# A hybrid block that starts on the residual before the norm between the two models: folded gains, two roots inside the first pair of weight chunks, sums of squares on VectorE, and one more weight chunk split ahead

## The reference, cut to what matters

```python
# end of first_block
h = h + conv_ffn(rmsnorm(h, f_norm_g[l]), ...)
x = rmsnorm(h, final_norm_g)                 # "fin1" in the kernel

# start of second_block
h = x
hn = rmsnorm_2(h, attn_norm[0])              # "at_norm0" in the kernel
proj = hn @ hyb_w_in[0]                      # 14 weight chunks, "hy"
qa, ka, va, rw = split(proj)                 # rw feeds rwkv7_time_mix
h = h + sb_rwkv_mixer(...)                   # needs x itself as the residual
```

## Time and profile before

| what | value |
|---|---|
| median of 3 runs | 1323.04 us (1322.97 to 1324.91) |
| the profiled execution | 1323.27 us, of which the profile's span is 1321.5 us |
| TensorE busy | 1300.0 us, 98% of the span |
| VectorE busy | 913.0 us, 69% |
| ScalarE busy | 758.1 us, 57% |
| GpSimd busy | 44.1 us, 3% |

### The profile page before, as it was taken

How to read it: one execution, slowest core, us unless ns; L and a number is a source line. 1 busy time by engine, 2 the same in 40 slices (tenths; PEclk the granted TensorE clock), 3 DMA queues, 4 the chain that set the end, 5 groups by cost and what they waited for, 6 DMA issues and landing times.

```text
span 1321.5 us, 29315 instructions
## 1 busy us (share of the span) xinstructions
PE 1300.0 (98%) x12222; PEld 1268.0 (96%) x12222; DVE 913.0 (69%) x1297; ACT 758.1 (57%) x977; POOL 44.1 (3%) x37
## 2 busy tenths in 40 slices
PE   9999999999999999999999999999999999999997
PEld 8999999998899999999989899999999889999997
DVE  4789886488479876468746387666578779666556
ACT  6667665367657665357554166554476876554444
POOL 1010000010010000010000010000001001000000
PEclk9999999999999999999999999999999999999999
DMA  8455555545345555535401135555435335555520
GB/s 333 175 208 191 191 190 191 191 191 195 125 160 191 191 190 191 191 122 191 160 34 37 65 136 211 182 184 199 179 141 187 130 128 200 192 190 190 191 96 33
DMA packets 31981, 220.63 MB, mean 167 GB/s; under 512 B 3712, under 2 KB 3840, under 8 KB 6160
## 3 DMA queue, kind: packets, MB, share of 16 engines
q1 hardware_dynamic: 30672, 213.36, 44.7%
q0 software_dynamic: 784, 4.85, 1.1%
q10 hardware_dynamic: 432, 1.05, 0.2%
HBM read 218.20 MB, written 1.05 MB: 166 GB/s over the span
## 4 chain that ended last, share of the span: by engine, by line
PE 87%; DVE 8%; ACT 3%; issue 1%; DMA 1%; POOL 0%; SPq 0%; DVEq 0%; ACTq 0%; POOLq 0%
PE ps L1850 22%; PE ps L1851 21%; PE ps L1852 21%; PE ps L1861 17%; DVE w_lo L1102 2%; PE ps L1856 2%; PE ps L1857 2%; PE ps L1858 2%; ACT w_hi L503 1%; DVE xt L1154 1%; PE ps L2072 1%; DMA raw<-stream 1%; DVE xA L1164 1%; DVE xB L1164 0%; DVE xB L1126 0%
## 5 line engine op out<-in xcount | busy, mean ns | idle before, releaser
L1102 DVE TENSOR_TENSOR w_lo<-raw,w_hi 128x2048 fp32r<-128x2048 f32 x197 | 449.9, 2288 | 149.3 <-ACT w_hi L503 148.8
L503 ACT ACTIVATE w_hi<-raw 128x2048 fp32r<-128x2048 f32 x197 | 376.2, 1913 | 169.8 <-PE ps L1852 165.4
L1850 PE MATMUL ps<-xB,w_hi 128*128 128x256 f32 x1120 | 314.4, 281 | 1.7 <-DVE up_acc L1228 1.7
L1852 PE MATMUL ps<-xB,w_lo 128*128 128x256 f32 x1120 | 312.7, 279 | 0.0
L1851 PE MATMUL ps<-xB,w_hi 128*128 128x256 f32 x1120 | 312.6, 279 | 0.0
L1850 PEld LDWEIGHTS ps<-xB,w_hi 128*128 128x128 f32 x1120 | 210.5, 188 | 3.1 <-DVE up_acc L1228 1.9
L1850 PE MATMUL ps<-xA,w_hi 128*128 128x256 f32 x744 | 210.7, 283 | 0.5 <-DVE w_lo L1102 0.5
L1851 PEld LDWEIGHTS ps<-xB,w_hi 128*128 128x128 f32 x1120 | 210.5, 188 | 0.1
L1852 PEld LDWEIGHTS ps<-xB,w_lo 128*128 128x128 f32 x1120 | 210.5, 188 | 0.0
L1851 PE MATMUL ps<-xA,w_hi 128*128 128x256 f32 x744 | 207.7, 279 | 0.0
L1852 PE MATMUL ps<-xA,w_lo 128*128 128x256 f32 x744 | 207.6, 279 | 0.0
(11 more groups left out here) (295 smaller groups left out, 1909.3 us busy)
## 6 DMA issues: line engine op xcount, KB each, us to landing
raw<-stream SPq DMA_DIRECT2D x199, 1024.0 KB, 4.8
raw<-stream SPq DMA_DIRECT2D x4, 512.0 KB, 7.6
at_bias<-rel POOLq DMA_DIRECT2D x1, 2048.0 KB, 8.1
hT<-x_t SPq DMA_DIRECT2D x4, 256.0 KB, 7.0
lora_w<-lora POOLq DMA_DIRECT2D x1, 1024.0 KB, 5.1
out_t<-xt SPq DMA_DIRECT2D x4, 256.0 KB, 2.4
hcon<-hyc POOLq DMA_DIRECT2D x1, 576.0 KB, 4.0
wsT<-wst ACTq DMA_DIRECT2D x1, 512.0 KB, 4.4
```

Source lines behind the costliest of these rows:

```text
L503: nc.scalar.activation(w_hi[c.slot][:], raw[c.slot][:], ACT.Copy).then_inc(hi_made, 1)
L1102: nc.vector.tensor_tensor(w_lo[c.slot][:], raw[c.slot][:], w_hi[c.slot][:].bitcast(F32), ALU.subtract).then_inc(lo_made, 1)
L1850: nc.tensor.matmul(out, wh, xh, start=start, stop=False, skip_group_check=True)
L1852: return nc.tensor.matmul(out, wl, xh, start=False, stop=stop, skip_group_check=True)
```

## The change

The separate norm `N_FIN1` goes. The hybrid block's pair and third chunk work on the old `hT` times `hy_gain`, the product of both norm weights. ScalarE makes two sets of squares for each quarter of `hT`: of `hT`, and of `hT * fin1` (eight more activations into `slot[2]` and `slot[3]`). VectorE adds both sets down (six additions; GpSimd adds nothing for this norm), TensorE sums both inside the pair, now at k = 6 rather than 5. The first root `fin_rs` comes from the first sum; VectorE multiplies the second sum by `fin_rs` squared; ScalarE takes the second root; VectorE multiplies the two roots into `rs`. The matmuls on ones go. `split_hi` and `split_lo` for `c0+4` move ahead of the block's evacuations, and the residual itself is normed (eight products into `hT`) between `with_eye(10, ...)` and `with_eye(14, ...)`.

```diff
-N_GM, N_FF0, N_AT, N_FF1, N_FIN1, N_HY, N_FF2, ... = range(12)
+N_GM, N_FF0, N_AT, N_FF1, N_HY, N_FF2, ... = range(11)
+POOLED = {n: 0 if n == N_HY else 2 if n in FOLDED else 1 for n in range(11)}
+        def early_gain(n, k):
+            return hy_gain[:, k:k + 1] if n == N_HY else col(EARLY[n][0], k)
 # GpSimd
-            add_squares(N_FIN1)
             pool.wait_ge(h_updated, 16)
...
-            add_squares(N_HY)
 # ScalarE
             ffn(1, N_FF1)
-            square_norm(N_FIN1)
             for b in range(4):
                 square(N_HY, b)
+                for k in (2 * b, 2 * b + 1):
+                    last = nc.scalar.activation(slot[2 + k // 4][:, k % 4, :], hT[:, k, :], ACT.Square, scale=col("fin1", k))
+                last.then_inc(fin_sq, 1)
             split_hi(Chunk(c0).ahead())
-            root_norm(N_HY)
+            act.wait_ge(ss_summed, N_HY + 1)
+            inverse_root(fin_rs[:], half(4, 0), D, fin_made)
+            act.wait_ge(fin_mean, 1)
+            inverse_root(rs[:], rs[:], 1, rs_made)
+            split_hi(Chunk(c0 + 1).ahead())
             round_x(OUT_HY, xA)
...
             act.wait_ge(mu_ready, 1)
-            split_hi(Chunk(c0 + 1).ahead())
             hy_copy(0)
 # VectorE, end of ffn
+                if n + 1 == N_HY:
+                    for b in (0, 4):
+                        dve.wait_ge(sq_made, 4 * N_HY + b // 2 + 2)
+                        own.mark(nc.vector.tensor_tensor(xt[:, b + 2:b + 4, :], xt[:, b + 2:b + 4, :], xt[:, b:b + 2, :],
+                                                         ALU.add))
+                    own.wait()
+                    nc.vector.tensor_tensor(xt[:, 6:8, :], xt[:, 6:8, :], xt[:, 2:4, :], ALU.add).then_inc(sq_folded, 1)
+                    dve.wait_ge(fin_sq, 4)
+                    for i in (2, 3):
+                        own.mark(nc.vector.tensor_tensor(slot[i][:, 0:2, :], slot[i][:, 0:2, :], slot[i][:, 2:4, :], ALU.add))
+                    own.wait()
+                    nc.vector.tensor_tensor(slot[2][:, 0:2, :], slot[2][:, 0:2, :], slot[3][:, 0:2, :],
+                                            ALU.add).then_inc(fin_folded, 1)
                 split_lo(Chunk(d0 + PAIRS - 1).ahead())
 # VectorE, around the hybrid block
+            link(nc.vector.tensor_tensor(hy_gain[:, 0:KD], col("fin1", 0, KD), col("at_norm0", 0, KD), ALU.mult))
             ffn(1, N_FF1)
-            root(N_FIN1)
-            for k in range(KD):
-                ins = nc.vector.scalar_tensor_tensor(out=hT[:, k, :], in0=hT[:, k, :], scalar=col("fin1", k), in1=rs[:],
-                                                     op0=ALU.mult, op1=ALU.mult)
-                ...
-            nc.vector.tensor_scalar(om_mu[:], ...).then_inc(mu_ready, 1)
-            dve.wait_ge(h_updated, 20)
-            for b in range(4):
-                rest_early(N_HY, b)
-            fold_squares(N_HY)
-            c0 = C0["hy"]
-            split_lo(Chunk(c0).ahead())
+            dve.wait_ge(fin_made, 1)
+            link(nc.vector.scalar_tensor_tensor(out=rs[:], in0=half(4, 1), scalar=1.0 / D, in1=fin_rs[:], op0=ALU.mult,
+                                                op1=ALU.mult))
+            nc.vector.tensor_tensor(rs[:], rs[:], fin_rs[:], ALU.mult).then_inc(fin_mean, 1)
+            split_lo(Chunk(c0).ahead())
+            nc.vector.tensor_scalar(om_mu[:], ...).then_inc(mu_ready, 1)
             root(N_HY)
+            link(nc.vector.tensor_tensor(rs[:], rs[:], fin_rs[:], ALU.mult))
             scale_x(OUT_HY, xA, "at_norm0")
+            split_lo(Chunk(c0 + 1).ahead())
...
             scale_early(N_HY, 2, c0 + 2, 2)
-            split_lo(Chunk(c0 + 1).ahead())
             shift(2)
...
             split_lo(Chunk(c0 + 12).ahead())
+            for k in range(KD):
+                nc.vector.scalar_tensor_tensor(out=hT[:, k, :], in0=hT[:, k, :], scalar=col("fin1", k), in1=fin_rs[:],
+                                               op0=ALU.mult, op1=ALU.mult).then_inc(fin_scaled, 1)
             with_eye(14, 7, -1)
 # TensorE, sum_folded and the block
-                plain(half(4, 0), ones, xt[:, 7, :], False, True).then_inc(ss_summed, 1)
+                last = plain(half(4, 0), ones, xt[:, 7, :], False, True)
+                if n == N_HY:
+                    pe.wait_ge(fin_folded, 1)
+                    plain(half(4, 1), ones, slot[2][:, 0, :], False, False)
+                    last = plain(half(4, 1), ones, slot[2][:, 1, :], False, True)
+                last.then_inc(ss_summed, 1)
...
-            keep_clock(10, 3)
-            sum_quarters(N_FIN1, range(4))
...
-                    early_pair(N_HY, Chunk(c0), Chunk(c0 + 1), 5)
+                    early_pair(N_HY, Chunk(c0), Chunk(c0 + 1), 6)
```

More of the change, by code:

```diff
@@ L75 @@
 OUT_GATED, OUT_FF0, OUT_KV, OUT_Q, OUT_FF1, OUT_HY, OUT_FF2, OUT_PL0, OUT_FF3, OUT_PL1 = range(10)
-N_GM, N_FF0, N_AT, N_FF1, N_FIN1, N_HY, N_FF2, N_PL0, N_ML, N_FF3, N_PL1, N_FIN2 = range(12)
+N_GM, N_FF0, N_AT, N_FF1, N_HY, N_FF2, N_PL0, N_ML, N_FF3, N_PL1, N_FIN2 = range(11)
 EARLY = {N_GM: ("a_norm", 4), N_FF0: ("f_norm0", 2), N_AT: ("kv_norm", 3), N_FF1: ("f_norm1", 2), N_HY: ("at_norm0", 3),
@@ L83 @@
 SCALED_AT = {n: sum(c for m, (_, c) in EARLY.items() if m < n) for n in EARLY}
-FOLDED = tuple(n for n in range(12) if n not in (N_FIN1, N_FIN2))
-ADDED_BY = {n: sum(2 if m in FOLDED else 1 for m in range(n)) for n in range(12)}
+FOLDED = tuple(range(N_FIN2))
+POOLED = {n: 0 if n == N_HY else 2 if n in FOLDED else 1 for n in range(11)}
+ADDED_BY = {n: sum(POOLED[m] for m in range(n)) for n in range(11)}
 FOLD_AT = {n: i for i, n in enumerate(FOLDED)}
 FINAL_XT = 8 * 10
-FILL = (3, 9)
 GATE_BANK = (4, 6, 7, 5)
@@ L143, in build @@
         rs = sb("rs", [P, T])
+        hy_gain = sb("hy_gain", [P, 4 * KD])
         with ExitStack() as f:
@@ L211, in build @@
                 om_mu = sb("om_mu", [P, 15], where=f)
+                fin_rs = sb("fin_rs", [P, T], where=f)
                 slot = [sb(f"slot{i}", [P, RBLK, T], where=f) for i in range(12)]
@@ L264, in build @@
         rs_made = sem("rs_made")
+        fin_sq, fin_folded, fin_made, fin_mean, fin_scaled = [
+            sem(n) for n in ("fin_sq", "fin_folded", "fin_made", "fin_mean", "fin_scaled")]
         xt_made = sem("xt_made")
@@ L477, in _ @@
             add_squares(N_FF2)
-            pool.wait_ge(h_updated, 24)
+            pool.wait_ge(h_updated, 20)
             pool.dma_start(pl_in[:], p_t[0]).then_inc(p_landed, 16)
@@ L486, in _ @@
             add_squares(N_FF3)
-            pool.wait_ge(h_updated, 36)
+            pool.wait_ge(h_updated, 32)
             pool.dma_start(pl_in[:], p_t[1]).then_inc(p_landed, 16)
@@ L1153, in scale_x @@
                 for k in range(KD):
-                    nc.vector.scalar_tensor_tensor(out=xt[:, k, :], in0=hT[:, k, :], scalar=col(gain, k), in1=rs[:],
+                    nc.vector.scalar_tensor_tensor(out=xt[:, k, :], in0=hT[:, k, :],
+                                                   scalar=early_gain(N_HY, k) if o == OUT_HY else col(gain, k), in1=rs[:],
                                                    op0=ALU.mult, op1=ALU.mult).then_inc(xt_made, 1)
@@ L1281, in ffn @@
                     rest_early(n + 1, 3)
-                if n + 1 in FOLDED:
+                if n + 1 in FOLDED and n + 1 != N_HY:
                     fold_squares(n + 1)
+                if n + 1 == N_HY:
[11 more added lines that the diff above has]
+                                            ALU.add).then_inc(fin_folded, 1)
                 split_lo(Chunk(d0 + PAIRS - 1).ahead())
@@ L1678, in _ @@
                 dve.wait_ge(chunk_used, co + g + 1)
+                if g == 0:
+                    dve.wait_ge(fin_scaled, KD)
                 add_quarter(g, 4 + g)
@@ L1870, in keep_clock, with sum_quarters @@
                     plain(ps[:, bank, 0:P], ones, ones)
-            def sum_quarters(n, quarters, idle=True):
+            def sum_quarters(n, quarters):
                 for b in quarters:
@@ L1879, in sum_quarters @@
                     else:
-                        if b == 3 and idle:
-                            keep_clock(FILL[0])
                         pe.wait_ge(sq_made, 4 * n + b + 1)
@@ L1886, in sum_quarters @@
                     last.then_inc(ss_summed, 1)
-                    if idle:
-                        keep_clock(FILL[1])
             in_halves = Chunk(0), Chunk(1)
@@ L2541, in _ @@
             keep_clock(12)
-            sum_quarters(N_FIN2, (2, 3), idle=False)
+            sum_quarters(N_FIN2, (2, 3))
 def _cols(v):
```

7 lines of the change are left out of this document (3 added, 4 removed).

## The result

The changed kernel takes 1331.35 us, the median of six runs (1327.48 to 1333.32), where the kernel before takes 1323.91 (1322.97 to 1324.91): a ratio of 1.0047, 95% interval 1.0033 to 1.0061. The forecast was 1317.1 us and faster. The profiled execution took 1327.48 us, its span is 1325.7. It is the fastest of the six: it lies 4.2 us above the profiled execution before, the median 7.4 us above the median before, so what follows accounts for 4.2 us and the rest of the median's loss is in no profile.

A forecast was written before the change was run, and what follows sets the result against it. TensorE, busy 98%, was taken to bound the kernel. Of 11.8 us without useful matmuls, gaps of 1.0, 1.5, 2.4 and a 0.7 sum return; 6.1 gained: 1323.27 - 6.1 = 1317.2, median 1317.1, range 1314.7 to 1319.1.

The forecast's parts named there:

- ScalarE's pace: First quarters of `hT`: two roundings, a square and two gained squares take ScalarE 2.16 us a quarter, setting the pace.
- `scale_x` held by the split of `c0+3`: Behind the roots: VectorE's `split_lo` of `c0+3`, 581.3 to 583.5, not the root, sets `scale_x` at 584.0, before 588.90.
- the split of `c0+4` between it and the banks: Behind `scale_x`: VectorE's `split_lo` of `c0+4` adds 2.2 us, so `scale_early` comes at 592.1, only 2.7 us earlier.
- the waits for the first and the fourth shift: TensorE: `c0+4` waits for the first shift until 594.6, the `lora_w` products for the fourth until 602.6.
- The eight late products: Products into `hT`, 3.25 us, done at 712.6: covered with 0.7 us left; with this placing they cost 0 to 1.
- the 6.04: Measured gain in us from the first quarter's addition to the `lora_w` products; the forecast for this stretch was 6.1.
- three gaps: TensorE's waits between second feed-forward and `lora_w` products, before the second sum, `c0+4` and those products: forecast 1.0, 1.5, 2.4 us.
- What is at no cost: Prediction's part on covered work: late products into `hT`, `hy_gain` (at most 0.2 us of `scale_early`'s delay), and transfers.
- the other side: Slower case: the clock falls at the third gap and stays at half; at 20 us it gives 1327; chance 0.04.
- a time between 602.6 and the block's end: Sign of being wrong: from the `lora_w` products to the hybrid block's end, times not the old ones moved by 6.1 us.
- no spell of half clock: TensorE's clock behind the new order's gaps: full clock assumed; one spell would cost 1.7 us, leaving 4.4 us gained.
- rival 1: One spell of half clock after the new order's third TensorE gap: 4.4 us gained, 1318.9; chance 0.12.

The follow-up runs named there:

- old_all_shifted: The kernel before with 128 unused bytes per partition ahead of the weight buffers, so weights and activations both lie 128 bytes higher; ratio 1.0006.
- old_96: The kernel before with 64 unused bytes behind the roots, so activations lie 96 bytes above the weights modulo 256; ratio 1.0199.
- new_again: The changed kernel repeated without alteration, beside the others on one chip; 1329.59 us, ratio 1.0051 to the kernel before.
- new_unshifted: The changed kernel with the `hy_gain` tile placed behind the hybrid block's slots, so no tile ahead of that block moves; 1321.15 us, ratio 0.9984.
- new_filled: new_unshifted with 26 small matmuls on ones in TensorE's three gaps; 1319.64 us, ratio 0.9971 to the kernel before.
- new_f17: new_unshifted with 17 small matmuls on ones in TensorE's three gaps (2, 5 and 10); 1320.03 us, ratio 0.9963 to the kernel before.
- new_f17_late9: new_f17 with nine more small matmuls on ones directly ahead of the third feed-forward; 1319.49 us, ratio 0.9961 to the kernel before.
- new_f17_mid9: new_f17 with nine more small matmuls on ones ahead of the first of the 64x64 products; 1319.89 us, ratio 0.9970 to the kernel before.

## Why the prediction was wrong

**What was right.** The chain of the changed place, step by step: ScalarE's pace, the pair without a gap at its start, the additions of 0.60 and 0.68 us, `scale_x` held by the split of `c0+3`, the split of `c0+4` between it and the banks, the waits for the first and the fourth shift. From the first addition `scale_x` starts at 19.65 us (forecast 584.0 - 564.28 = 19.7) and the banks are scaled at 27.69 (27.8). The eight late products were covered: VectorE still waits 0.49 us for TensorE behind them (forecast 0.7).

```profile
708.97 3.25 DVE L1644 SCALAR_TENSOR_TENSOR hT<-hT,vec,fin_rs 128x256 f32<-128x256 f32 x8
712.71 0.69 DVE L1622 SCALAR_TENSOR_TENSOR slot<-ps,hcon 128x512 f32<-128x512 f32 x1 [0.49 <-PE ps L1886]
```

**Where the 6.04 was luck.** It holds for this pair of executions. The one before has a spell of half clock at the old place, and the one of the changed kernel has none behind its three gaps. Of the seven profiles with the old order and its filler, three have that spell (the kernel before, `old_all_shifted`, `old_96`) and reach the products with `lora_w` 44.5 to 45.3 us behind the first addition; the other four stay at full clock and need 43.1 to 43.8, at tile distances that make their matmuls slower. So more than 1 us of the 6.04 is the old spell, which doesn't come each time.

**The step that failed** is in "What is at no cost": "`hy_gain` is one product of eight columns". That priced the instruction and put the tile at nothing. The whole sum rested on rows outside the changed place staying as they were; the tile's 128 bytes made TensorE slower in them, by 7.1 us in the profiled execution (2.98 + 0.51 + 1.04 + 0.89 + 0.42 + 1.27 of the table), more than the 6.04 gained, of which the block kept 4.00. Between the executions timed, the shift costs the old program 1.0094 and the new one 1.0051 / 0.9984 = 1.0067. The forecast's range allowed for none of it, and no rival had it; the other side was given to a clock that stays at half, which no run showed.

**A smaller miss** is "a time between 602.6 and the block's end that isn't the old one moved by 6.1 us", which the prediction named as a way to be wrong and gave no price. In the changed kernel's execution an `issue` gap of 1.76 us stands at 715.74, where no work was added to TensorE; a second profile of the same kernel, `new_again`, has 0.55 there. In the profiled `new_unshifted` such a gap of 2.03 us with the half clock behind it, the third feed-forward's 1.5 us and the start's 1.3 us make up most of what it lies above the forecast. How the 4 us between the median of 1321 and the forecast of 1317 are shared among them, one profile doesn't show.

**The clock.** I took no spell of half clock, since the earlier trace rows had a gap of 2.03 us that full clock followed. That row was one draw: the same gap in the same first stage is followed by half clock (0.79 on the mean from 64 to 72 us) in 10 of 17 profiled executions, and costs some 1.4 us (from the gap's end to the first feed-forward 20.99 us in `new_unshifted` and `new_filled`, 19.62 before). In `new_filled` from 66 to 70:

```profile
66.00:70.00 4.00, 4.00 (x24) 4.00 (x23) 4.00 (x3) 1.56 (x2) 0.00 (x0) 0.57 0.48 145
```

Behind the third gap of the new order half clock came in 2 of the 5 executions that leave it open, and in none of the 4 that fill it. By these few draws rival 1 deserved nearer 0.4 than 0.12. The two `issue` gaps of 1.76 and 2.03 us differ in the same way: full clock behind the first, half behind the second. The Trainium skill (TensorE: Matmul & The Clock Gate, Part 1: The HAM clock gate) has the throttled clock as the default that activity lifts; these executions agree with it in that the idle stretches are where it falls, though not each time.

**The best version** of these is the changed order with the tile out of the way and fillers that fit: `new_f17`, 0.9963. It is 0.4% faster than the kernel before; `new_f17_late9`, `new_f17_mid9` and `new_filled` can't be told from it within their intervals.

## What to carry to other kernels

A new tile is a change to every tile made behind it. Before an edit to a kernel bound by TensorE is judged, compare the count of matmuls in a stretch that the edit doesn't touch, or put new small tiles behind all others; otherwise 128 bytes can hide a gain of several us. A row that shows what the clock did behind one gap is one draw: price the spell by how often it comes.

## What the runs showed of the hardware that was not expected

The pace of float32 matmuls (128x128 weights, 256 columns) depends on where the moving tile lies against the weight tiles modulo 256 bytes, at the full clock and with TensorE never waiting: 165 us of the first feed-forward hold 1417 matmuls at a distance of 32, 1393 at 160, 1377 at 0 and at 96. The distance is not all: at 160 a start-to-start time of 118.67 ns was seen in some feed-forwards and 117.33 in others. On the whole kernel that is up to 2%. The Trainium skill (SBUF — State Buffer, SBUF: two separate sides) says that only the port pair shared by VectorE and GpSimd causes contention on the engines' side; it has no rule on addresses by which these counts would differ, and the measurement stands. Whether two reads of TensorE itself meet, or TensorE and another engine, no run here tells.

TensorE can stand still in a stage of short matmuls without a wait that the profile shows: gaps of 0.30 to 2.27 us put down to issue, in the 64x64 products, present or absent by the count of instructions ahead of them. The Trainium skill (Runtime: NRT & Kernel Launch, Instruction fetch mechanics) calls the cost of crossing a block of instructions mostly hidden; if these gaps are such crossings, it isn't always in this stage. For that speak the positions and the instruction transfers of 16 KB that start 2.2 to 2.4 us ahead of the longest gap's end in all eight profiles that have one. It is argued, not shown.
